# Two token-major projections in 512 columns, the second branch's gates ahead of the first branch's projection, and the attention heads six steps later

## The chip, the core and the metric

The kernel runs on one core of a Trainium2 chip. TensorE (PE) does the matrix products into eight banks of PSUM, ScalarE (ACT) and VectorE (DVE) move and transform the results, GpSimd (POOL) does some elementwise work that must not touch PSUM, and SyncE (SP) issues most of the DMA transfers. The metric is the device time of one execution in microseconds, the median of several runs. Only the order and the shape of work change here, not what is computed.

## The reference

Two transformer blocks over 256 tokens of width 1024, in fp32. The change touches the first block's mixer, cut here to what matters:

```python
hn = rmsnorm(h, norm_mix)
proj = hn @ w_in                      # 1024 x (many splits)
(fq, fk, fv, ff, gq, gk, gv, ga, gb, gz, gate_fox, gate_gdn) = split_in(proj)
y_fox = fox_attention(fq, fk, fv, log_sigmoid(ff + bias))     # 8 heads of 128, causal, forget gates
qkv = silu(causal_dwconv(concat(gq, gk, gv), gdn_conv_w))
o = gated_delta_rule(l2norm(q), l2norm(k), v, g, beta)         # 8 heads of 128
y_gdn = rmsnorm(o, gdn_norm) * silu(gz)
y = sigmoid(gate_fox) * (y_fox @ w_branch_fox) + sigmoid(gate_gdn) * (y_gdn @ w_branch_gdn)
h = h + y @ w_out
```

A feed-forward block with a short convolution follows, and then the second transformer block.

## The kernel before

Every weight matrix is read in **panels** of 1 MB (8 tiles of 128 rows by 256 columns, or 4 tiles of 128 rows by 512 columns). `panels()` writes the list `PLAN` out by hand, and its order is the order of the program. SyncE fetches a panel into one of three raw buffers. Each panel is worked on in two halves, the **steps**: there are 252, numbered n = 1 to 252, and everything is placed by n. To keep fp32 precision each half is split: ScalarE rounds it to `panel_hi` (L1019), VectorE subtracts to get `panel_lo` (L1469), and TensorE multiplies three times (high by high, low by high, high by low) in `gemm(n)` (L551). ScalarE's split of step n waits until TensorE has finished step n-4.

A panel has one of these forms. "fm" gives the product with features on partitions, "tm" with tokens on partitions: both are 24 matmuls of 256 columns in a step. "wide" gives tokens on partitions and 512 columns: 12 matmuls in a step, with two banks for a product. The gate `z` (z of `gz`) and the first attention's values `fv` are "tm" before; both have the normalised input `x_halves` as the stationary operand in either form.

All five engine programs are loops over n, and what an engine does beside the panels is hung on a step by conditions such as `if n == 68`. An engine works strictly in the order of its program. In the order of the program the steps before are: k, q, v, z for the delta rule (1 to 32); `fq`, `fk`, `fv` by turns (33 to 56); `gate_f` (57 to 64); `branch_f`, the projection of the first branch (65 to 72); `gate_g` (73 to 80); `branch_g` (81 to 88); `out` (89 to 96).

Hung on them, and named in the prediction:

- **The heads of the first attention**, from `FOX_AT = {39 + 3*hh: hh}`. For head hh with step s: TensorE computes the scores at s; VectorE adds `key_bias` and takes the maximum at s+1 (L1701); ScalarE exponentiates at s+2, and then issues the DMA load of the next head's key bias (L545, L546); VectorE normalises at s+3 (L1709, L1712); TensorE turns the probabilities at s+4 (`fox_turn`, L839) after waiting for that; TensorE multiplies by the values at s+5 (`fox_values`); ScalarE and VectorE split the result into `yf_hi` and `yf_lo` (L1717) at s+5. GpSimd adds the causal mask to head hh+1's `key_bias` (L2134) at its own position s+1, waiting for that load to land. There is one `key_bias` buffer.
- **The inversion of 16x16 blocks** for the delta rule: TensorE forms keys by keys at n = 38, VectorE inverts row by row from n = 42 to 47, the result goes to DRAM and back into `X` and `XT` (SyncE, n = 48), and TensorE needs `X` at n = 52 (`px_16`).
- **The solve** at n = 63 (`solve_first`, `solve_rest`), which gives `o_tok`. ScalarE squares it at n = 64, VectorE sums at 65 and takes the mean at 66; at n = 66 GpSimd raises the mean to the power -1/2 (L2129) and multiplies `o_tok` by `gz` (L2181); VectorE waits for this at n = 68, scales `o_tok` (L2006), and TensorE turns it at n = 71 (L674). GpSimd also scales and shifts the gates (L2140): `gate_f` at 58 to 64, `gate_g` at 74 to 80.
- **Banks.** Products up to `gate_f` use the ring "few" (banks 0 and 1), attention heads the ring "fox" (banks 2 and 3), later products the ring "gemm" (banks 0 to 3). A user of a bank waits until the one before it is emptied.

Of the kernel before, what the change touches and what calls it, by code (L numbers as in the profile page):

```python
# [19 lines left out]
ALU = mybir.AluOpType  # L20
# [50 lines left out]
for _name, _n in (("ident", P), ("upper", P), ("ones", 4), ("causal", P), ("decay_mask", P),  # L71
# [7 lines left out]
CONV_ORDER = [("k", 2), ("z", 0), ("k", 3), ("q", 0), ("z", 1), ("q", 1), ("q", 2), ("z", 2),  # L79
              ("q", 3), ("v", 0), ("z", 3), ("v", 1), ("v", 2), ("v", 3)]  # L80
# [8 lines left out]
def panels():  # L89
# [11 lines left out]
    for kind, j in CONV_ORDER:  # L101
# [49 lines left out]
SEQ = [("k", 0), ("k", 1)] + CONV_ORDER  # L151
CONVS = [p for p in SEQ if p[0] != "z"]
COPY_AT = {p: END[p] for p in SEQ} | {("k", 0): 4, ("k", 1): 5}
# [4 lines left out]
FOX_AT = {39 + 3 * hh: hh for hh in range(HEADS)}  # L158
# [31 lines left out]
def build(nc, a, out, scratch_a, scratch_x, scratch_c):  # L190
    ctx = ExitStack()
    with ctx:
# [35 lines left out]
        nwT = at("nwT", [P, HEADS, P], 11)  # L228
        S1 = at("S1", [P, HEADS, DH], 11.5)
# [8 lines left out]
        gate_g = at("gate_g", [P, KD, T], 18)  # L238
# [248 lines left out]

        def side(key):
            return bank_for("side", key)
# [59 lines left out]
        def tensor_program(e):  # L549
# [5 lines left out]
            def gemm(n):  # L555
# [286 lines left out]
            def fox_values(hh):  # L842
# [5 lines left out]
                e.wait_ge(*emptied(("fv", hh // 2)))  # L848
# [88 lines left out]
            for n in range(1, STEPS + 1):  # L937
# [41 lines left out]
                if n - 5 in FOX_AT and FOX_AT[n - 5] < 7:  # L979
# [8 lines left out]
                if n == 64:  # L988
                    fox_values(7)
# [27 lines left out]
        def scalar_program(e):  # L1017
# [101 lines left out]
            def z_tanh(j):  # L1119
                m = SEQ.index(("z", j))  # L1120
                tmp_free(m)
                e.wait_ge(*product(("z", j)))
                e.activation(conv_tmp[m % 4], pairs(bank_of(("z", j))), ACT.Tanh, scale=0.5).then_inc(s_gz_tanh, 1)
# [171 lines left out]
            for n in range(1, STEPS + 1):  # L1295
# [82 lines left out]
                if n - 5 in FOX_AT and FOX_AT[n - 5] < 7:  # L1378
# [7 lines left out]
                for j in range(4):  # L1386
# [10 lines left out]
                    if n == END["gate_g", j]:  # L1397
                        e.wait_ge(*emptied(("o1", 0)))
# [5 lines left out]
                if n == 64:  # L1404
                    fox_hi(7)
# [55 lines left out]
        def vector_program(e):  # L1461
# [74 lines left out]
            def z_silu(j, order):  # L1536
                e.wait_ge(s_gz_tanh, order)
                e.scalar_tensor_tensor(gz[:, :, col2(j)], conv_tmp[SEQ.index(("z", j)) % 4], 1.0,
                                       pairs(bank_of(("z", j))), ALU.add, ALU.mult).then_inc(empties(("z", j)), 1)
# [351 lines left out]
            for n in range(1, STEPS + 1):  # L1891
# [53 lines left out]
                if n in Z_AT:  # L1945
                    z_silu(Z_AT[n], Z_AT[n] + 1)
# [68 lines left out]
                if n - 5 in FOX_AT and FOX_AT[n - 5] < 7:  # L2015
# [19 lines left out]
                if n == 64:  # L2035
                    fox_lo(7)
# [346 lines left out]
```

## Time and profile before

| | us |
|---|---|
| median of 3 runs | 818.33 |
| lowest of 3 runs | 816.98 |
| the profiled execution | 817.55 |
| its span | 816.2 |

The profiled execution lies 0.78 us under the median. 1.35 us of it lie outside the span that the trace covers. TensorE is busy for 99% of the span, VectorE for 72%, ScalarE for 55% and GpSimd for 9%. So the time is close to what TensorE's instructions take one after another, and a microsecond counts where TensorE does less work or waits less. The granted clock is at its full level in the whole profile.

### The profile page before, as it was taken

Reading aid. Unit: us, or ns where it says so; the run is one execution under the profiler, and the core shown is the slowest. Engines: PE = TensorE matmul, PEld = TensorE weight load, DVE = VectorE, ACT = ScalarE, POOL = GpSimd, SP = SyncE. Lnnn points to the kernel's source line nnn. Section 1 sums busy time; section 2 is a strip of 40 time slices with the busy share of each in tenths; the row PEclk is TensorE's granted clock in tenths of the full one; section 3 lists DMA queues with packets and bytes.
Section 4 is the critical chain, followed back from the end, with each engine's and each line's share of the span. In section 5 each row is a group of like instructions: output and inputs, shape, how many; then the busy total and the mean of one; then the engine's idle time right before and its main releaser. Section 6 shows DMA issues by size and latency. Waiting matters only on the chain.

```text
span 816.2 us, 14536 instructions
## 1 busy us (share of the span) xinstructions
PE 804.7 (99%) x5910; PEld 738.6 (90%) x5910; DVE 589.5 (72%) x967; ACT 446.9 (55%) x721; POOL 76.6 (9%) x67
## 2 busy tenths in 40 slices
PE   7999999999999999999999999999999999999998
PEld 5999999999999999899999998888777888888886
DVE  6878878785553746669999997486766777777543
ACT  5666577654454444455656563456664656555441
POOL 0001000001010401100211011012100111011000
PEclk9999999999999999999999999999999999999999
DMA  8754663646440564575687766555424666565541
GB/s 261 234 172 143 192 223 109 181 136 186 116 134 31 163 199 162 200 232 167 198 244 223 240 199 208 185 185 177 155 78 132 207 203 203 173 192 193 192 162 72
DMA packets 130194, 144.18 MB, mean 177 GB/s; under 512 B 11456, under 2 KB 110928, under 8 KB 129872
## 3 DMA queue, kind: packets, MB, share of 16 engines
q1 hardware_dynamic: 127680, 141.19, 54.6%
q10 hardware_dynamic: 2448, 2.05, 1.0%
q8 instruction: 47, 0.77, 0.4%
q14 instruction: 19, 0.16, 0.1%
HBM read 141.78 MB, written 1.46 MB: 175 GB/s over the span
## 4 chain that ended last, share of the span: by engine, by line
PE 94%; DVE 2%; DMA 1%; ACT 1%; issue 0%; POOL 0%; ACTq 0%; DVEq 0%; POOLq 0%
PE bank L551 92%; DVE panel_lo L1469 1%; DMA panel_raw<-in_w_in 1%; PE bank L597 1%; DMA h<-in_x 1%; PE bank L889 0%; PE bank L619 0%; ACT panel_hi L1019 0%; PE bank L839 0%; DVE blocks_T L1628 0%; DVE decayT L1532 0%; PE bank L862 0%; PE bank L674 0%; DVE x_halves L1490 0%; DVE blocks_X L1631 0%
## 5 line engine op out<-in xcount | busy, mean ns | idle before, releaser
L1469 DVE TENSOR_TENSOR panel_lo<-panel_raw,panel_hi 128x1024 fp32r<-128x1024 f32 x252 | 319.3, 1270 | 153.4 <-ACT panel_hi L1019 153.1
L551 PE MATMUL bank<-x_halves,panel_hi 128*128 128x256 f32 (+1 forms) x1952 | 415.3, 304 | 1.7 <-DVE x_halves L1490 1.5
L1019 ACT ACTIVATE panel_hi<-panel_raw 128x1024 fp32r<-128x1024 f32 x252 | 266.6, 1059 | 176.7 <-PE bank L551 171.4
L551 PEld LDWEIGHTS bank<-x_halves,panel_hi 128*128 128x128 f32 x1952 | 315.3, 191 | 17.1 <-DVE panel_lo L1469 1.7
L551 PE MATMUL bank<-x_halves,panel_lo 128*128 128x256 f32 x1152 | 324.8, 282 | 0.0
L551 PEld LDWEIGHTS bank<-x_halves,panel_lo 128*128 128x128 f32 x1152 | 219.8, 191 | 0.0
L551 PE MATMUL bank<-panel_hi,x_halves 128*128 128x256 f32 (+1 forms) x384 | 88.1, 324 | 0.0
L551 PEld LDWEIGHTS bank<-panel_hi,x_halves 128*128 128x128 f32 x384 | 63.4, 190 | 5.8 <-issue 0.7
L551 PE MATMUL bank<-panel_hi,act_hi 128*128 128x512 f32 x176 | 68.6, 390 | 0.0
L551 PE MATMUL bank<-panel_hi,act_lo 128*128 128x512 f32 x176 | 68.5, 389 | 0.0
L551 PE MATMUL bank<-panel_lo,act_hi 128*128 128x512 f32 x176 | 68.5, 389 | 0.0
L551 PE MATMUL bank<-panel_lo,x_halves 128*128 128x256 f32 (+1 forms) x192 | 61.2, 319 | 0.0
L551 PEld LDWEIGHTS bank<-panel_hi,act_hi 128*128 128x128 f32 x176 | 33.0, 188 | 6.9
L551 PEld LDWEIGHTS bank<-panel_lo,act_hi 128*128 128x128 f32 x176 | 33.0, 188 | 6.9
L551 PEld LDWEIGHTS bank<-panel_hi,act_lo 128*128 128x128 f32 x176 | 33.0, 188 | 6.7
L551 PEld LDWEIGHTS bank<-panel_lo,x_halves 128*128 128x128 f32 x192 | 36.5, 190 | 2.6
L2129 POOL TENSOR_TENSOR stats<-stats 128x2 f32<-128x2 f32 (+1 forms) x9 | 17.1, 1906 | 190.1 <-DVE stats L1483 104.8
L1503 DVE SCALAR_TENSOR_TENSOR conv_acc<-conv_tmp,params,conv_acc 128x255 f32<-128x255 f32 (+2 forms) x72 | 30.2, 476 | 0.0
L2154 POOL TENSOR_TENSOR ff_tanh<-ff_tanh,ff_val 128x512 f32<-128x512 f32 x11 | 17.2, 1565 | 112.4 <-DVE ff_tanh L1780 112.4
L2161 POOL TENSOR_TENSOR f_tanh<-f_tanh,ff_val 128x512 f32<-128x512 f32 x11 | 14.3, 1299 | 108.3 <-DVE f_tanh L1856 108.3
L2134 POOL TENSOR_TENSOR key_bias<-key_bias,constants 128x128 f32<-128x128 f32 x16 | 8.9, 577 | 151.2 <-DMA key_bias<-gate_sums 151.2
L1774 DVE SCALAR_TENSOR_TENSOR ff_gate<-ff_raw,params,ff_gate 128x255 f32<-128x255 f32 (+1 forms) x44 | 21.3, 543 | 0.0
(284 smaller groups left out, 973.3 us busy)
## 6 DMA issues: line engine op xcount, KB each, us to landing
panel_raw<-in_w_in SPq DMA_DIRECT2D x38, 1024.0 KB, 5.3
panel_raw<-in_w_up SPq DMA_DIRECT2D x30, 1024.0 KB, 5.3
panel_raw<-in_w_down SPq DMA_DIRECT2D x20, 1024.0 KB, 5.1
panel_raw<-in_w_gate SPq DMA_DIRECT2D x10, 1024.0 KB, 5.3
panel_raw<-in_w_out SPq DMA_DIRECT2D x8, 1024.0 KB, 5.1
panel_raw<-in_w_in SPq DMA_DIRECT2D x12, 512.0 KB, 4.6
panel_raw<-in_w_branch_fox SPq DMA_DIRECT2D x4, 1024.0 KB, 5.2
panel_raw<-in_w_branch_gdn SPq DMA_DIRECT2D x4, 1024.0 KB, 5.1
```

The costliest lines, as they stand in the source:

```text
L551: return e.matmul(o, l, r, start=start, stop=stop, skip_group_check=True)
L597: i_ = e.transpose(b3[:, k, m * P:(m + 1) * P], h[:, m, f * P:(f + 1) * P], ident)
L1019: return e.activation(o, i_, ACT.Copy, scale=scale)
L1469: e.tensor_tensor(lo, raw_view(i, k0, kt), hi.bitcast(F32), ALU.subtract).then_inc(s_lo, 1)
L1503: e.scalar_tensor_tensor(acc[:, f, back:], tmp[:, f, 0:T - back], gconv(p, f, back), acc[:, f, back:], ALU.mult, ALU.add).then_inc(s_taps, 1)
L1774: e.scalar_tensor_tensor(acc[:, c, back:], raw_[:, c, 0:T - back], fconv(s, j, c, back), acc[:, c, back:], ALU.mult, ALU.add).then_inc(s_f ...
L2129: return e.tensor_tensor(cols, cols, minus_half.broadcast_to([P, n]), ALU.pow)
L2134: i_ = e.tensor_tensor(key_bias[:, s], key_bias[:, s], C("causal"), ALU.add)
L2154: e.tensor_tensor(th, th, ff_acc[j % 2][1], ALU.mult).then_inc(s_f_mul, 1)
L2161: e.tensor_tensor(th, th, ff_acc[j % 2][1], ALU.mult).then_inc(s_g_mul, 1)
```

## The change

The panels of `z` and of `fv` become "wide": four panels each of 4 row tiles by 512 columns, in the place of four panels of 8 row tiles by 256. The `z` panels keep their places among steps 7 to 26, and the products end at steps 14 and 26. The `fv` panels move in front of all of `fq` and `fk`, to steps 33 to 40. `fq` and `fk` follow at 41 to 56. Since queries and keys now end later, all heads start six steps later, at 45 to 66. `gate_g` moves in front of `branch_f`: `gate_g` has steps 65 to 72, `branch_f` 73 to 80. The last head, which ended with `fox_values(7)` at n = 64 directly behind its turn at n = 64, is now in the regular pattern (turn at 70, values at 71). The two matrices `nwT` and `S1` and the buffer `gate_g` change places in SBUF, so that `gate_g` no longer waits for the solve. A wide product takes two banks, and the wait for the second one stands just in front of the matmuls that write it.

```diff
-CONV_ORDER = [("k", 2), ("z", 0), ("k", 3), ("q", 0), ("z", 1), ("q", 1), ("q", 2), ("z", 2),
-              ("q", 3), ("v", 0), ("z", 3), ("v", 1), ("v", 2), ("v", 3)]
+CONV_ORDER = [("k", 2), ("z", 0), ("k", 3), ("q", 0), ("z", 0), ("q", 1), ("q", 2), ("z", 1),
+              ("q", 3), ("v", 0), ("z", 1), ("v", 1), ("v", 2), ("v", 3)]
...
-        add((kind, j), "mix", kind != "z", "w_in", 0, KD, c0 + j * PW)
+        if kind == "z":
+            add_wide((kind, j), "mix", "w_in", HALF * CONV_ORDER[:i].count((kind, j)), HALF, c0 + j * WIDE)
+        else:
+            add((kind, j), "mix", True, "w_in", 0, KD, c0 + j * PW)
+    for j in range(2):
+        for k in (0, HALF):
+            add_wide(("fv", j), "mix", "w_in", k, HALF, C_FV + j * WIDE)
     for j in range(4):
-        for kind, c0 in (("fq", C_FQ), ("fk", C_FK), ("fv", C_FV)):
-            add((kind, j), "mix", kind != "fv", "w_in", 0, KD, c0 + j * PW)
-    for kind, x, w, c0 in (("gate_f", "mix", "w_in", C_GF), ("branch_f", "yf", "w_branch_fox", 0),
-                           ("gate_g", "mix", "w_in", C_GG), ("branch_g", "yg", "w_branch_gdn", 0)):
+        for kind, c0 in (("fq", C_FQ), ("fk", C_FK)):
+            add((kind, j), "mix", True, "w_in", 0, KD, c0 + j * PW)
+    for kind, x, w, c0 in (("gate_f", "mix", "w_in", C_GF), ("gate_g", "mix", "w_in", C_GG),
+                           ("branch_f", "yf", "w_branch_fox", 0), ("branch_g", "yg", "w_branch_gdn", 0)):
...
-FOX_AT = {39 + 3 * hh: hh for hh in range(HEADS)}
+FOX_AT = {45 + 3 * hh: hh for hh in range(HEADS)}
...
-        nwT = at("nwT", [P, HEADS, P], 11)
-        S1 = at("S1", [P, HEADS, DH], 11.5)
+        nwT = at("nwT", [P, HEADS, P], 12)
+        S1 = at("S1", [P, HEADS, DH], 12.5)
...
-        gate_g = at("gate_g", [P, KD, T], 18)
+        gate_g = at("gate_g", [P, KD, T], 11)
...
+        def ring_of(key):
+            if key[0] == "z" or key in (("fv", 0), ("fq", 0), ("fk", 0)):
+                return "fox"
+            return "few" if END[key] <= END["gate_g", 3] else "gemm"
...
-                        bank_for("few" if n <= END["gate_f", 3] else "gemm", target)
-                        for s, v in room(target):
-                            e.wait_ge(s, v)
+                        bank_for(ring_of(key), target)
...
+                    if first and j < len(targets):
+                        for s, v in room(targets[j]):
+                            e.wait_ge(s, v)
...
-                e.wait_ge(*emptied(("fv", hh // 2)))
+                for m in range(TT):
+                    e.wait_ge(*emptied(("fv", hh // 4, m)))
...
-                if n - 5 in FOX_AT and FOX_AT[n - 5] < 7:
+                if n - 5 in FOX_AT:
                     fox_values(FOX_AT[n - 5])
...
-                if n == 64:
-                    fox_values(7)
...
-                        e.wait_ge(*emptied(("o1", 0)))
                         gate("gate_g", j, gate_g)
...
-                    if n == END["fv", j]:
-                        e.wait_ge(*product(("fv", j)))
-                        e.tensor_copy(vf[:, :, col2(j)], pairs(bank_of(("fv", j)))).then_inc(empties(("fv", j)), 1)
+                    if j < 2 and n == END["fv", j]:
+                        for m in range(TT):
+                            e.wait_ge(*product_of(("fv", j), m))
+                            e.tensor_copy(vf[:, m, wide(j)], bank_of(("fv", j, m))).then_inc(empties(("fv", j, m)), 1)
```

`z_tanh` (ScalarE) and `z_silu` (VectorE) do in the same way two instructions of 512 elements at n = 14 and two at n = 26, in the place of one at each of 8, 14, 20 and 26. Lines of the changed kernel are 14 to 16 numbers higher than those of the kernel before.

Three places where the order of an engine's instructions changes. First **GpSimd**, from the keys' norms to the second branch's gates. `key_bias` x2 is one head's mask, the `stats` row of 16 is the power, `o_tok` the multiplication by `gz`. Before:

```order
L2129 TENSOR_TENSOR stats<-stats 128x16
L2134 TENSOR_TENSOR key_bias<-key_bias,constants 128x128 x16
L2140 TENSOR_SCALAR gate_f<-gate_f 128x512 x4
L2129 TENSOR_TENSOR stats<-stats 128x16
L2181 TENSOR_TENSOR o_tok<-o_tok,gz 128x8x128 x2
L2140 TENSOR_SCALAR gate_g<-gate_g 128x512 x4
```

After:

```order
L2144 TENSOR_TENSOR stats<-stats 128x16
L2149 TENSOR_TENSOR key_bias<-key_bias,constants 128x128 x12
L2155 TENSOR_SCALAR gate_f<-gate_f 128x512 x2
L2149 TENSOR_TENSOR key_bias<-key_bias,constants 128x128 x2
L2155 TENSOR_SCALAR gate_f<-gate_f 128x512
L2149 TENSOR_TENSOR key_bias<-key_bias,constants 128x128 x2
L2155 TENSOR_SCALAR gate_f<-gate_f 128x512
L2144 TENSOR_TENSOR stats<-stats 128x16
L2197 TENSOR_TENSOR o_tok<-o_tok,gz 128x8x128 x2
L2155 TENSOR_SCALAR gate_g<-gate_g 128x512 x4
```

The masks of heads 6 and 7 have moved between the scalings of `gate_f`: the last one now stands behind two of them, and right in front of the last scaling and the power.

Second **VectorE**, from its step 65 on (before) and from its step 67 on (after), around the scaling of `o_tok`. `panel_lo` is the split of the next panel. Before:

```order
L1469 TENSOR_TENSOR panel_lo_60<-panel_raw_52,panel_hi_56 128x1024
L1996 TENSOR_REDUCE stats<-o_squares 128x8 x2
L1469 TENSOR_TENSOR panel_lo_57<-panel_raw_50,panel_hi_53 128x1024
L2000 SCALAR_TENSOR_TENSOR stats<-stats 128x16
L1724 TENSOR_TENSOR gate_f<-bank,gate_f 128x512
L1469 TENSOR_TENSOR panel_lo_58<-panel_raw_50,panel_hi_54 128x1024
L1469 TENSOR_TENSOR panel_lo_59<-panel_raw_51,panel_hi_55 128x1024
L2006 TENSOR_TENSOR o_tok<-o_tok,stats 128x1024 x2
L1724 TENSOR_TENSOR gate_f<-bank,gate_f 128x512
L1469 TENSOR_TENSOR panel_lo_60<-panel_raw_51,panel_hi_56 128x1024
```

After:

```order
L1483 TENSOR_TENSOR panel_lo_58<-panel_raw_50,panel_hi_54 128x1024
L1717 ISA fox_p_70,stats<-bank,key_bias 128x128
L1717 ISA stats 128x1
L1717 ISA fox_p_70,stats<-bank,key_bias 128x256
L1717 ISA stats 128x1
L1483 TENSOR_TENSOR panel_lo_59<-panel_raw_51,panel_hi_55 128x1024
L2022 TENSOR_TENSOR o_tok<-o_tok,stats 128x1024 x2
L1733 TENSOR_TENSOR yf_lo<-bank,yf_hi 128x256
L1483 TENSOR_TENSOR panel_lo_60<-panel_raw_51,panel_hi_56 128x1024
L1725 RECIPROCAL stats<-stats 128x2
L1728 TENSOR_SCALAR fox_p_70<-fox_p_70,stats 128x128
L1728 TENSOR_SCALAR fox_p_70<-fox_p_70,stats 128x256
```

Behind the scaling of `o_tok` there now follow head 6's `yf_lo`, a split, and the normalising of head 7 (RECIPROCAL and two TENSOR_SCALAR); before, all heads were done by then and only the products with `gate_f` followed.

Third **TensorE**, at the turn of head 7 (`fox_p_70`), which is after step 64 before and after step 70 now. Before:

```order
L551 MATMUL bank<-x_halves,panel_hi_56 128x256 x2
L551 MATMUL bank<-x_halves,panel_lo_60 128x256
L839 MATMUL bank<-constants,fox_p_70 128x128 x3
L551 MATMUL bank<-fox_pT_73,vf 128x128 x3
L551 MATMUL bank<-yf_hi,panel_hi_53 128x256
L551 MATMUL bank<-yf_lo,panel_hi_53 128x256
L551 MATMUL bank<-yf_hi,panel_lo_57 128x256
```

After:

```order
L566 MATMUL bank<-x_halves,panel_hi_54 128x256 x2
L566 MATMUL bank<-x_halves,panel_lo_58 128x256
L855 MATMUL bank<-constants,fox_p_70 128x128 x3
L566 MATMUL bank<-x_halves,panel_hi_55 128x256 x2
L566 MATMUL bank<-x_halves,panel_lo_59 128x256
```

The values of head 7 stood directly behind its turn; now a step of 24 matmuls and the turns of `o_tok` lie between them, and the turn itself stands six steps later, in front of the panel of `gate_g`.

## Rows read from the trace of the kernel before

**Rows 1.** The page: busy time, and shares of the chain that ended last.

```profile
PE 804.7 (99%) x5910; PEld 738.6 (90%) x5910; DVE 589.5 (72%) x967; ACT 446.9 (55%) x721; POOL 76.6 (9%) x67
...
PE 94%; DVE 2%; DMA 1%; ACT 1%; issue 0%; POOL 0%; ACTq 0%; DVEq 0%; POOLq 0%
```

**Rows 2.** Two stretches: length, busy time (count) of PE, PEld, DVE, ACT, POOL; PEclk, DMA.

```profile
400.00:480.00 80.00, 80.00 (x669) 80.00 (x668) 77.39 (x114) 47.77 (x70) 10.02 (x7) 1.00 0.74 227
760.00:810.00 50.00, 50.00 (x222) 41.41 (x221) 23.10 (x20) 17.59 (x18) 0.63 (x1) 1.00 0.43 141
```

**Rows 3.** Waits of TensorE over the whole span.

```profile
PE bank L619 <- DVE conv_tmp L1509: 1.0, 1, 1.0
PE bank L551 <- DVE stats L1701: 0.7, 1, 0.7
```

**Rows 4.** Timeline of TensorE: start, duration, instruction, idle before.

```profile
1.43 5.63 PE L551 MATMUL bank<-zeros 128*128 128x512 f32 x8 [1.43 <-DVE zeros L1863]
8.81 1.09 PE L597 MATMUL bank<-constants,h 128*128 128x128 f32 x8 [1.75 <-DVE h L1880]
...
188.98 2.06 PE L551 MATMUL bank<-X,BT 64*64 64x32 f32 x64
...
230.40 0.92 PE L551 MATMUL bank<-kfT,qfT 128*128 128x128 f32 x4
...
234.03 0.49 PE L839 MATMUL bank<-constants,fox_p 128*128 128x128 f32 x3
...
237.23 0.83 PE L551 MATMUL bank<-fox_pT,vf 128*128 128x128 f32 x6
...
240.78 1.06 PE L551 MATMUL bank<-tok_v,XT 128*128 128x128 f32 x8
...
259.54 0.49 PE L839 MATMUL bank<-constants,fox_p 128*128 128x128 f32 x3
260.78 0.91 PE L551 MATMUL bank<-fox_pT,vf 128*128 128x128 f32 x6 [0.75 <-issue]
```

**Rows 5.** Timeline of GpSimd, 225 to 277 us.

```profile
230.54 0.87 POOL L2134 TENSOR_TENSOR key_bias<-key_bias,constants 128x128 f32<-128x128 f32 x2 [12.47 <-DMA key_bias<-gate_sums]
231.38 1.30 POOL L2140 TENSOR_SCALAR gate_f<-gate_f 128x512 f32<-128x512 f32 x2
...
267.87 2.91 POOL L2129 TENSOR_TENSOR stats<-stats 128x16 f32<-128x16 f32 x1 [6.00 <-DVE stats L2000]
270.75 5.76 POOL L2181 TENSOR_TENSOR o_tok<-o_tok,gz 128x1024 f32<-128x1024 f32 x2
```

**Rows 6.** ScalarE issues the last key bias load; landing times of L546.

```profile
225.65 0.33 ACTq L545 DMA_DIRECT2D key_bias<-gate_sums  x1
...
DMA to landing us min/median/max: 4.3/4.5/7.2
```

**Rows 7.** Timeline of VectorE, 242 to 282 us.

```profile
242.56 0.15 DVE L1709 RECIPROCAL stats<-stats 128x2 f32<-128x2 f32 x1
242.75 0.55 DVE L1712 TENSOR_SCALAR fox_p<-fox_p,stats 128x128 f32<-128x128 f32 x2
...
262.14 0.42 DVE L1717 TENSOR_TENSOR yf_lo<-bank,yf_hi 128x256 fp32r<-128x256 f32 x1 [2.48 <-ACT yf_hi L1019]
...
276.61 2.36 DVE L2006 TENSOR_TENSOR o_tok<-o_tok,stats 128x1024 f32<-128x1024 f32 x2 [2.37 <-POOL o_tok L2181]
...
279.48 2.35 DVE L1469 TENSOR_TENSOR panel_lo<-panel_raw,panel_hi 128x1024 fp32r<-128x1024 f32 x2
```

**Rows 8.** VectorE around the block inversion, and the DMA issues behind it.

```profile
154.34 0.29 DVE L1960 TENSOR_SCALAR blocks_A<-blocks_A 128x256 f32<-128x256 f32 x1 [1.10 <-DMA blocks_A<-blocks_to_invert]
...
173.45 0.39 DVE L1970 COPY blocks_T<-blocks_X 128x256 f32<-128x256 f32 x1
...
L2278 SPq DMA_DIRECT2D X<-blocks_inverted x8: 319/448/450, 181.4 to 184.7; - x8
...
X<-blocks_inverted SPq DMA_DIRECT2D x8, 16.0 KB, 3.7
```

More of the change, by code:

```diff
@@ L149 @@
 FIRST_HALF = {p[0]: min(n for n, (i, _, _) in enumerate(HALVES) if PLAN[i][0] == p[0]) for p in PLAN}
-SEQ = [("k", 0), ("k", 1)] + CONV_ORDER
+SEQ = [("k", 0), ("k", 1)] + [q for i, p in enumerate(CONV_ORDER) if p not in CONV_ORDER[i + 1:]
+                              for q in ([(*p, m) for m in range(TT)] if p[0] == "z" else [p])]
 CONVS = [p for p in SEQ if p[0] != "z"]
-COPY_AT = {p: END[p] for p in SEQ} | {("k", 0): 4, ("k", 1): 5}
+COPY_AT = {p: END[p[:2]] for p in SEQ} | {("k", 0): 4, ("k", 1): 5}
 CONV_AT = {COPY_AT[p]: c for c, p in enumerate(CONVS)}
@@ L1119, in z_tanh @@
             def z_tanh(j):
[L1120 to L1123, printed above, removed]
+                for m in range(TT):
+                    i_ = SEQ.index(("z", j, m))
+                    tmp_free(i_)
+                    e.wait_ge(*product_of(("z", j), m))
+                    e.activation(conv_tmp[i_ % 4].rearrange("p c t -> p (c t)"), bank_of(("z", j, m)), ACT.Tanh, scale=0.5) \
+                        .then_inc(s_gz_tanh, 1)
             def turned(name, dst, b):
@@ L1377, in scalar_program @@
                              units(bank_of(("yg", b))), PR("gdn_norm")).then_inc(s_yg_hi, 1)
-                if n - 5 in FOX_AT and FOX_AT[n - 5] < 7:
+                if n - 5 in FOX_AT:
                     fox_hi(FOX_AT[n - 5])
@@ L1403, in scalar_program @@
                     px_32()
-                if n == 64:
-                    fox_hi(7)
                 for x, kind, gain, first in (("ffn", "out", "norm_ffn", 2), ("norm1", "down", "norm1", 4),
@@ L1534, in decay, with z_silu @@
                 i_.then_inc(s_dec_sub, 1)
[L1536 to L1539, printed above, removed]
+            def z_silu(j):
+                for m in range(TT):
+                    e.wait_ge(s_gz_tanh, 2 * j + m + 1)
+                    tanh = conv_tmp[SEQ.index(("z", j, m)) % 4].rearrange("p c t -> p (c t)")
+                    e.scalar_tensor_tensor(gz[:, m, wide(j)], tanh, 1.0, bank_of(("z", j, m)), ALU.add, ALU.mult) \
+                        .then_inc(empties(("z", j, m)), 1)
             def gates_1():
@@ L1945, in vector_program @@
                 if n in Z_AT:
-                    z_silu(Z_AT[n], Z_AT[n] + 1)
+                    z_silu(Z_AT[n])
                 if n == 38:
@@ L2014, in vector_program @@
                                                ALU.subtract).then_inc(empties(("yg", b)), 1)
-                if n - 5 in FOX_AT and FOX_AT[n - 5] < 7:
+                if n - 5 in FOX_AT:
                     fox_lo(FOX_AT[n - 5])
@@ L2021, in vector_program @@
                 for j in range(4):
-                    if n == END["fv", j]:
-                        e.wait_ge(*product(("fv", j)))
-                        e.tensor_copy(vf[:, :, col2(j)], pairs(bank_of(("fv", j)))).then_inc(empties(("fv", j)), 1)
+                    if j < 2 and n == END["fv", j]:
+                        for m in range(TT):
+                            e.wait_ge(*product_of(("fv", j), m))
+                            e.tensor_copy(vf[:, m, wide(j)], bank_of(("fv", j, m))).then_inc(empties(("fv", j, m)), 1)
                     if n == min(END["branch_g", j] + 1, END["branch_g", 3]) and j < 3:
@@ L2034, in vector_program @@
                     px_32()
-                if n == 64:
-                    fox_lo(7)
                 if n == 63:
@@ L2177, in pool_program @@
                     e.wait_ge(s_osq, 2)
-                    for j in range(4):
-                        e.wait_ge(*emptied(("z", j)))
+                    for j in range(2):
+                        for m in range(TT):
+                            e.wait_ge(*emptied(("z", j, m)))
                     for m in range(TT):
```

2 lines of the change are left out of this document (1 added, 1 removed).

## The prediction

> **What bounds the kernel now.** I read the page first. TensorE is busy for 804.7 us of the 816.2 us span, and 94% of the chain that ended last are its own instructions [rows 1]. So TensorE is the bound nearly everywhere, and there are only two ways to move the time: make its work shorter, or change how long it waits. The other engines matter where they make it wait. The list of waits says how little there is to win: in the steps that change, the longest are one of 1.0 us for `conv_tmp` and one of 0.7 us for `stats` L1701 [rows 3], and a few under 1 us that have no engine's name. Next I read what a step costs in each form. In 80 us of 256-column steps there lie 669 matmuls, in 50 us of 512-column steps 222 [rows 2]. Such a count takes in two or three matmuls that only reach into the stretch, so the true distance from one to the next is a little over 80/669 and 50/222: 0.120 and 0.227 us, with the count corrected by 2. Last I read the timelines of the four engines between 225 and 282 us, where the last heads, the solve and the scaling of `o_tok` meet [rows 4 to 7], and around the block inversion [rows 8].
>
> **Part 1, 512 columns.** A step of 24 matmuls by 0.120 is 2.88 us, one of 12 by 0.227 is 2.72 us [rows 2]. The bytes, the splits and the columns stay equal: only 12 fixed costs of a matmul go. 16 steps (8 of `z`, 8 of `fv`) by 0.16 us give **-2.5 us**. In both stretches TensorE is busy all the time and the weights' loading (80.00 of 80, 41.41 of 50) does not hold it, with `x_halves` or the other operand as the stationary one; I take the 0.16 whole. The bounds are nothing and -2.5. The Trainium skill, in "TensorE: Matmul & The Clock Gate", section "Wait — 56ns, not 53.3ns?", puts a warm matmul at its columns over 2.4 GHz plus about 2.5 ns. By that a step of either form would take 2.62 or 2.59 us and this part would give 0.5 us, not 2.5; the trace has some 13 ns over the columns for each matmul, so it does not agree, and the measured distance is used.
>
> **Part 2, evacuations.** The four tanh and four products of `z` are 512 elements each, as before, but two fall together at n = 14 and at n = 26; the same with the copies of `fv`, at 36 and 40. They are not on TensorE and the panels run several microseconds ahead. One place is thinner: TensorE waits 1.0 us for the gated `conv_tmp` at n = 37 [rows 3], where VectorE works without a break. VectorE's chain is set off by the turns of step 33, TensorE comes four short steps sooner: I add +0.1 us, at most +0.6. The changed order of the banks costs nothing: each bank has at least four steps between its uses.
>
> **Part 3, the heads six steps on.** Six is a multiple of three, so between steps 45 and 63 the same kind of head work stands in each step as before, only of a head two lower. TensorE's work for a head is the same wherever it stands. From the starts in the timeline: scores to turn 3.63, turn to values 3.20, values to the next 3.55 us, each with a step of 2.88 in it, so 0.75 + 0.32 + 0.67 = 1.74 us [rows 4]. What changes is where it waits.
> - Head 7's turn and values stood back to back after step 64: the turn took 1.24 us to the start of the values, which waited 0.75 for the copy of the turned probabilities, where a turn costs 0.32 [rows 4]. Now a step lies between. That gives **-0.9 us**.
> - The wait of 0.7 us for `stats` L1701 [rows 3] came from a head's bias queued on VectorE behind the inversion (n = 46), at 171 us. The head work in the inversion's steps is now less, so I take it as gone: **-0.7 us** (bounds 0 and -0.7).
> - The inversion's results must be back when TensorE reaches `px_16` at 188.98 [rows 4]. TensorE will be there sooner by 2.5 + 0.7 and by the work of two heads, 3.3 to 3.5 us: about 6.4 us. The way back starts sooner as well: VectorE spent 154.34 to 173.45 on the inversion [rows 8], and in it 3.3 us on heads 0 and 1 and on a copy of `fv`, which are no longer there; with another 2 us for the start (a shorter way to the keys by keys, one copy of `fv` less in front of them) the result leaves 5.3 us sooner. The way back, through DRAM, ended with the eighth issue of `X` at 184.7 and 3.7 us for its landing [rows 8]: `X` was back at 188.4, 15 us after the inversion, with 0.6 us to spare. 0.6 + 5.3 - 6.4 is -0.5 at the middle. I take **+0.3 us**, between 0 and +2.
>
> **Part 4, the new wait.** This decides. I count from the start of the solve, 240.78 [rows 4], as 0; up to there all engines keep their distances. Step 64 ends at 18.8 (259.54), and with head 6's scores now behind the solve at 19.4. TensorE would go on: turn 5, step 65 to 22.6; values 5, step 66 to 26.2; scores 7, step 67 to 29.7; turn 6, step 68 to 32.9; values 6, step 69 to 36.4; step 70 to 39.3. There it wants to turn head 7, for which VectorE must have normalised it.
> - VectorE stands still before that, at n = 68, until GpSimd has multiplied `o_tok` by `gz` (it idles 2.37 us for it even now) [rows 7]. Behind that wait are queued the scaling of `o_tok`, `yf_lo` of head 6, the split of step 72 and only then the normalising of head 7.
> - GpSimd in turn has got head 7's mask in front of the power. The load of that key bias is issued when ScalarE reaches the values of head 5, at 22.6 + 0.7 = 23.3; the mask began 4.9 us after the issue (225.65 to 230.54), as soon as both halves had landed [rows 5, 6], so at 28.2. With 0.87 for the mask and 0.65 for one scaling of `gate_f` the power can start at 29.7, where its own input would allow 27.3 (27.1 before, and 0.2 for the heads' work on VectorE). The power takes 2.9 (267.87 to 270.75), the two products 5.76 [rows 5]: 38.4.
> - VectorE then: 2.36 for `o_tok`, 0.35 of the 0.42 for `yf_lo`, 1.17 for the split, 0.65 for reciprocal and two scalings [rows 7] (each but the last up to where the next begins): 43.0.
> TensorE waits from 39.3 to 43.0: **+3.7 us**. The lower bound is no mask in the way: 2.4 less, +1.3. The upper: the second half of such a load landed after 4.5 us in the median and after 7.2 at most [rows 6]; with 7.2 the wait is +6.4. Nothing is late behind it: the split of step 72 is done at 42.3 and wanted at 46; `yf_lo` of head 7 at about 50.5 and wanted for step 74, at 54. The squares of `o_tok` come as early as before against the solve.
>
> **Part 5, gates.** `gate_g` runs the same matmuls in the same form 8 steps sooner, with ScalarE's tanh in the place of VectorE's products. Its scaling on GpSimd stands behind the multiplication of `o_tok`, as before. Nothing waits: 0, covered by the eight steps of `branch_f` until `branch_g` wants it.
>
> **The sum.** -2.5 + 0.1 - 0.9 - 0.7 + 0.3 + 3.7 = 0.0. On the profiled execution's 817.55 us (span 816.2 and 1.35 outside) that is 817.6; its own median is 818.33, 0.8 above it. I forecast 818.0, between the two: **no change**, what the wide panels give being taken back by the wait at head 7's turn. A difference of under 2% (16 us) can't be told from none.
>
> **Rivals.**
> - *The wait is hidden* (chance 0.22). If GpSimd's chain is done some 3 us sooner, or VectorE starts `o_tok` sooner, TensorE finds head 7 ready: 817.6 - 3.7, about 814. For it: two of GpSimd's numbers are rough, and the power's 2.9 us may be start-up. Against it: even without the mask the chain ends 1.3 us too late.
> - *The load of the key bias lands late* (0.13), on the other side: VectorE's wait grows one for one with the landing. At 7.2 us in the place of 4.5 it gives 817.6 + 2.7 = 820.3, and the kernel is slower than before as soon as the load needs half a microsecond more than in the median. For it: one of the loads here did need 7.2 [rows 6]. Against it: the last one, in the same traffic of panels, was at the median.
> - *The clock falls* (0.10). A wait of 3.7 us would be the longest of TensorE. In this trace it waited up to 1.75 us with the clock still at its full level, 2.4 GHz, after [rows 4]. Only the first matmuls, after nothing, were slow: 5.63 us for 4 products of 512 columns, while four products of 128 columns take 1.06 us with the last one's tail [rows 4], so that four of 512 should take about 4. A drop to 1.2 GHz would then cost some 1.7 us: 819.3. The same page of the Trainium skill, section "What's actually happening", has the array fall back to 1.2 GHz after enough idleness; no row here shows such a fall.
> - *Wide steps give nothing* (0.05): if the half as many matmuls keep the same total, as the columns do, the 2.5 us are missing: 817.6 + 2.5 = 820.1. Against it speak the two counts of rows 2, made in the same kernel. (By the Trainium skill's rule of part 1, same page, 0.5 of them would be left and the time 819.6.)
>
> **How the numbers follow.** The forecast's case (a wait of 2.5 to 5.5 us, 816 to 819.5) has 0.50. The range takes in the hidden wait below and the late load above, with 0.8 us between median and profiled run at the top: 813.5 to 821.5. All cases lie within 2% (802 to 835): same 0.98, and 0.01 on each side for what I have not seen.
>
> **What the profile would show.** 12 matmuls in 2.72 us in the steps of `z` and `fv`. TensorE idle for 3 to 5 us in front of the `fox_p` turn that stands one step ahead of the turns of `o_tok`, ended by VectorE L1728, with GpSimd's mask late in front of its power. No 0.75 us wait in front of the last values. At `px_16` a wait under 2 us. I am wrong if there is no such wait, or if a wait of several microseconds stands elsewhere, above all at `px_16` or in front of a panel.

## The result, and the profile after

The changed kernel takes 821.11 us in the median of 6 runs (820.67 to 822.02), the kernel before 817.65 in the median of the 5 beside them (816.98 to 819.08), with one execution of 1600.22 left out (817.99 with it). The ratio is 1.004, with a 95% interval of 1.0028 to 1.0051: over 3 us slower. That is inside 2%, but outside what the runs scatter. The profiled execution took 820.71 us, with a span of 819.4.

The page of the changed kernel, its busy times and the chain that ended last; then three lines from the list of TensorE's waits (us in total, times, longest), the longest and those at the places of [rows 3] and of px_16:

```profile
PE 804.2 (98%) x5718; PEld 729.9 (89%) x5718; DVE 589.2 (72%) x967; ACT 446.8 (55%) x721; POOL 76.2 (9%) x67
...
PE 88%; issue 4%; DVE 3%; DMA 3%; POOL 1%; ACT 1%; SPq 0%; ACTq 0%; POOLq 0%; DVEq 0%
```

```profile
PE bank L855 <- DVE fox_p L1728: 4.9, 1, 4.9
...
PE bank L635 <- DVE conv_tmp L1523: 1.3, 1, 1.3
...
PE bank L566 <- DMA X<-blocks_inverted: 0.3, 1, 0.3
```

The wait that was forecast is there, at the turn of head 7, and it is now the longest of TensorE by far: 4.9 us. Against [rows 1], TensorE's part of the chain falls from 94% to 88%. Of these six points GpSimd and VectorE have taken one each and DMA two; the 4% of "issue" are not lost time but mostly one piece of 25.99 us, in which the chain runs through GpSimd's idle time in front of head 7's mask while TensorE works. The chain around that place shows in which order (start, length, what):

```profile
238.87 25.99 issue
...
264.90 0.09 POOL key_bias L2149
...
265.31 0.46 POOL key_bias L2149
265.77 0.59 POOL gate_f L2155
266.37 2.87 POOL stats L2144
269.23 4.76 POOL o_tok L2197 x2
...
274.08 3.10 DVE o_tok L2022 x2
277.18 0.34 DVE yf_lo L1733
277.52 1.13 DVE panel_lo L1483
278.65 0.09 DVE stats L1725
...
278.76 0.56 DVE fox_p L1728 x2
...
279.45 0.69 PE bank L855 x3
```

The timeline of TensorE from px_16 to the turns of `o_tok`. The solve, which answers to 240.78 in [rows 4], starts at 235.03, px_16 (188.98 there) at 183.09:

```profile
183.09 2.06 PE L566 MATMUL bank<-X,BT 64*64 64x32 f32 x64 [0.28 <-DMA X<-blocks_inverted]
...
235.03 1.06 PE L566 MATMUL bank<-tok_v,XT 128*128 128x128 f32 x8
...
274.23 0.28 PE L566 MATMUL bank<-x_halves,panel_lo 128*128 128x256 f32 x1
279.45 0.69 PE L855 MATMUL bank<-constants,fox_p 128*128 128x128 f32 x3 [4.95 <-DVE fox_p L1728]
279.80 0.78 PE L566 MATMUL bank<-x_halves,panel_hi 128*128 128x256 f32 x2
280.37 0.41 PE L566 MATMUL bank<-x_halves,panel_lo 128*128 128x256 f32 x1
...
283.12 0.40 PE L566 MATMUL bank<-x_halves,panel_hi 128*128 128x256 f32 x2
283.36 0.28 PE L566 MATMUL bank<-x_halves,panel_lo 128*128 128x256 f32 x1
...
284.19 1.91 PE L690 MATMUL bank<-constants,o_tok 128*128 128x128 f32 x16
```

Behind the wait, from 279.80 to 283.12, the matmuls stand 0.21 us apart; from 283.12 on it is the usual 0.12. The windows of the same place show why (length; busy and count of PE, PEld, DVE, ACT, POOL; granted clock; DMA):

```profile
278.00:280.00 2.00, 0.55 (x4) 0.58 (x5) 1.97 (x5) 0.00 (x0) 0.00 (x0) 0.91 0.09 22
280.00:282.00 2.00, 2.00 (x11) 2.00 (x11) 0.44 (x1) 1.75 (x3) 0.62 (x1) 0.50 0.99 343
282.00:284.00 2.00, 2.00 (x15) 2.00 (x14) 1.23 (x1) 0.17 (x1) 0.00 (x0) 0.73 0.46 160
284.00:286.00 2.00, 2.00 (x20) 2.00 (x20) 0.46 (x1) 1.18 (x3) 0.00 (x0) 1.00 0.71 226
```

The granted clock is 0.50, 1.2 GHz, from the end of the wait until about 283.1 (what the windows lack to 1.00 adds up to 3.4 us at half the clock). Where the time went is read from the end of each step (the moment at which TensorE reports its products), before and after, side by side. The changed kernel is 0.12 us late after step 1, 1.16 ahead after step 26 (all of `z`), 5.75 ahead after step 57, 4.46 ahead after step 70, with head 7's turn and values (0.99 us) still to come. Step 71 then takes 9.84 us; with 2.88 for its products and 0.32 for the turn it would be 3.20. The 6.64 us over are 4.95 of waiting and 1.69 behind it. From step 72 to the end the distance stays between 3.1 and 3.2.

### The profile page after: what moved, and what is told of

It is laid out like the page before. It is cut to its first block, busy times and chain, and to the rows that moved or that the text cites. A ratio compares the mean times of both kernels' runs of the same rounds, so it can differ in the third digit from the quotient of the medians.

```text
span 819.4 us, 14145 instructions
## 1 busy us (share of the span) xinstructions
PE 804.2 (98%) x5718; PEld 729.9 (89%) x5718; DVE 589.2 (72%) x967; ACT 446.8 (55%) x721; POOL 76.2 (9%) x67
## 4 chain that ended last, share of the span: by engine, by line
PE 88%; issue 4%; DVE 3%; DMA 3%; POOL 1%; ACT 1%; SPq 0%; ACTq 0%; POOLq 0%; DVEq 0%
PE bank L566 85%; DVE panel_lo L1483 1%; DMA blocks_inverted<-blocks_X 1%; PE bank L613 1%; DMA h<-in_x 1%; POOL o_tok L2197 1%; DMA X<-blocks_inverted 1%; DMA key_bias<-gate_sums 1%; PE bank L906 0%; PE bank L635 0%; POOL stats L2144 0%; DVE o_tok L2022 0%; ACT panel_hi L1034 0%; SPq L2294 0%; DVE blocks_T L1644 0%
## 5 line engine op out<-in xcount | busy, mean ns | idle before, releaser
L566 PE MATMUL bank<-panel_hi,x_halves 128*128 128x512 f32 x256 | 80.6, 396 | 0.0
L566 PEld LDWEIGHTS bank<-panel_hi,x_halves 128*128 128x128 f32 x256 | 46.8, 188 | 9.9 <-DVE panel_lo L1483 0.6
L566 PE MATMUL bank<-panel_lo,x_halves 128*128 128x512 f32 x128 | 50.0, 391 | 0.0
L566 PEld LDWEIGHTS bank<-panel_lo,x_halves 128*128 128x128 f32 x128 | 24.0, 188 | 5.2
```

The source lines that it names most:

```text
L566: return e.matmul(o, l, r, start=start, stop=stop, skip_group_check=True)
```

## The experiments

The profiles differ in their start: step 1 ends at 14.6 to 14.9 us in seven of the twelve traces and at 16.1 to 16.3 in five. Most of that is TensorE's clock. It starts on `x_halves` at 11.4 to 11.8 us in all of them, but in the five the granted clock is at 0.50 for 3.4 us around that start. The kernel without wide `z` of the last experiment shows it:

```profile
8.90 1.09 PE L607 MATMUL bank<-constants,h 128*128 128x128 f32 x8 [2.12 <-DVE h L1886]
11.52 0.68 PE L560 MATMUL bank<-x_halves,panel_hi 128*128 128x256 f32 x2 [1.52 <-DVE x_halves L1496]
```

```profile
10.00:12.00 2.00, 0.48 (x3) 0.51 (x4) 1.98 (x5) 2.00 (x5) 0.00 (x0) 0.91 1.00 314
12.00:14.00 2.00, 2.00 (x11) 2.00 (x11) 1.99 (x5) 1.88 (x4) 0.00 (x0) 0.50 0.00 1
```

So each experiment at head 7 is read from step 71 alone, and the medians stand beside it. The table holds all of them; the last column is what is left of step 71 when the idle time and the extra products are taken from it and the 3.20 us of its own work too.

| kernel | median, runs | ratio to before, interval | step 71 | extra products | idle | clock after | left |
|---|---|---|---|---|---|---|---|
| changed | 821.11 (6) | 1.0040, 1.0028 to 1.0051 | 9.84 | 0 | 4.95 | 0.50 | 1.69 |
| scaling behind | 816.20 (11) | 0.9978, 0.9970 to 0.9987 | 4.82 | 0 | 1.42 | 1.00 | 0.20 |
| power in front | 818.49 (12) | 1.0005, 0.9995 to 1.0016 | 5.98 | 0 | 2.60 | 1.00 | 0.18 |
| 36 extra | 830.80 (4) | 1.0154, 1.0140 to 1.0167 | 18.75 | 15.55 | 0 | 1.00 | 0 |
| 15 extra | 821.13 (5) | 1.0035, 1.0022 to 1.0048 | 9.67 | 6.47 | 0 | 1.00 | 0 |
| 8 extra | 820.14 (8) | 1.0033, 1.0019 to 1.0047 | 8.31 | 3.5 | 1.45 | 1.00 | 0.2 |
| 4 extra | 822.23 (5) | 1.0044, 1.0032 to 1.0056 | 9.61 | 1.7 | 3.17 | 0.50 | 1.5 |
| both orders | 815.49 (5) | 0.9966, 0.9954 to 0.9978 | 3.20 | 0 | 0 | 1.00 | 0 |

**The scaling of `o_tok` behind the normalising of head 7.** VectorE's block of n = 68 (wait for `s_ogz`, scaling) is moved:

```diff
-                if n == 68:
+                if n == 69:          # now below fox_normalise and fox_bias
                     e.wait_ge(s_o_rs, 1)
                     e.wait_ge(s_ogz, 2)
```

> The changed kernel with one edit: VectorE's scaling of o_tok (which waits for GpSimd's product with gz) stands behind the normalising of head 7 instead of in front of it. Theory A (the whole loss is the 4.95 us of idle TensorE in front of the turn of head 7, together with the lower clock that follows it): step 71 goes from 9.84 us to 3.2, nothing is late behind it (the scaling ends near 277.2, its turn is reached near 277.7), and the time falls by 4.95 + 1.69 = 6.6 us, to about 814.1 for the profiled execution and 814.5 in the median, 0.996 of the kernel before. Rival B (the wait moves on to the turn of the scaled o_tok, since the scaling now stands behind two more pieces of work): half or more of the 6.6 us stays, 817 to 820. Rival C (the slow clock belongs to this place and not to the wait): only 4.95 us come back, about 816.2.

Measured: 816.20, and step 71 shorter by 5.02 us, not 6.64. The slow stretch is gone with the long wait, against rival C. Rival B did not happen either: nothing waits at the turn of `o_tok`. A wait of 1.42 us stayed, at the same turn, for a reason that no theory named. VectorE and GpSimd in that kernel:

```profile
274.60 0.15 DVE L1725 RECIPROCAL stats<-stats 128x2 f32<-128x2 f32 x1
274.79 2.86 DVE L1728 TENSOR_SCALAR fox_p<-fox_p,stats 128x128 f32<-128x128 f32 x2
```

```profile
271.18 5.74 POOL L2197 TENSOR_TENSOR o_tok<-o_tok,gz 128x1024 f32<-128x1024 f32 x2
276.89 1.24 POOL L2155 TENSOR_SCALAR gate_g<-gate_g 128x512 f32<-128x512 f32 x2
```

The two small scalings take 2.86 us where they took 0.55 [rows 7]: VectorE stands until GpSimd's product is over, at 276.92. Without these 2.31 us head 7 would have been ready before TensorE wanted it, at 276.4. The Trainium skill, in "SBUF — State Buffer", section "Who interferes with whom", says that the two engines share a pair of ports, that a scaling by a scalar can take both of VectorE's, and that whoever comes second is blocked until the other's instruction is done. The trace agrees, with 2.86 us for 0.55.

**The power in front of the mask.** On GpSimd:

```diff
+    mask_key_bias(7)                 # in the block of n == 66, behind power(...)
-    if n - 1 in FOX_AT and FOX_AT[n - 1] + 1 < HEADS:
+    if n - 1 in FOX_AT and FOX_AT[n - 1] + 1 < HEADS - 1:
```

> The changed kernel with one edit on GpSimd: the power for o_tok stands in front of the mask of head 7, and no longer waits for the load of that key bias. The prediction put the share of the mask and its load at 2.4 us. From the trace of the changed kernel: the power's input is there at 262.1 and it starts at 266.3; it would start at 262.1, end at 265.0, mask to 265.9, gate_f to 266.5, the products to 271.3, and head 7 would be normalised near 276.5. Theory A: the wait shrinks from 4.95 to about 2 us; as no wait of up to 1.75 us was followed by a lower clock, the clock stays full and 1.7 us more come back: 820.7 - 3.0 - 1.7 = 816.0 (817.7 if the clock falls all the same). Rival B (GpSimd is not what VectorE waits for): no change, 821.

Measured: a wait of 2.60 us, the clock at 1.00 behind it, step 71 shorter by 3.86. GpSimd is what VectorE waits for, and the mask and its load in front of the power made the wait 2.35 us longer (4.95 less 2.60), even after the 1.0 us by which the products are slower here. The median, 818.49, fell by 2.6 only, over a wide scatter of 12 runs (816.80 to 822.08). That fits a clock that sometimes falls behind this wait too: one stretch of 3.4 us at half the clock takes 0.002 off the mean granted clock, the traces have at most one such stretch at the start, and four of the 12 executions have a mean of 0.993 to 0.996. They took 819.09 to 822.08 us, the four with a mean of 1.00 took 816.80 to 818.11. Where their clock fell isn't shown, since only the profiled execution has a trace. GpSimd's rows in this kernel:

```profile
263.60 2.91 POOL L2144 TENSOR_TENSOR stats<-stats 128x16 f32<-128x16 f32 x1 [5.44 <-DVE stats L2016]
266.47 0.88 POOL L2149 TENSOR_TENSOR key_bias<-key_bias,constants 128x128 f32<-128x128 f32 x2
267.31 5.76 POOL L2198 TENSOR_TENSOR o_tok<-o_tok,gz 128x1024 f32<-128x1024 f32 x2
273.04 2.17 POOL L2155 TENSOR_SCALAR gate_g<-gate_g 128x512 f32<-128x512 f32 x2
```

The products take 5.76 us again, as before the change; in the changed kernel, where VectorE does nothing beside them, 4.78.

**Extra products in the wait.** In front of TensorE's wait for the normalised head 7:

```diff
+                if hh == 7:
+                    for _ in range(36):      # 15, 8, 4 in the others
+                        mm(bank[:, 0:T], qfT[:, hh, 0:P], kfT[:, hh, :])
                 e.wait_ge(s_fox_norm, hh + 1)
```

> The changed kernel with 36 extra products of TensorE (qfT by kfT of head 7, 256 columns, overwritten by the turn that follows) in front of its wait for the normalised head 7; they compute nothing that is used. The work and the wait of the other engines are unchanged. Theory A (after the idle stretch TensorE runs at 1.2 GHz for some 3.5 us, which costs 1.7 us): the turn starts at the same time, near 279.4, but at full clock, and the time falls by 1.7, to 819.4 in the median. Rival B (the slow stretch comes from something else, for example the panel transfers that start again together): the granted clock still falls after 279.4 and the time stays at 821.1.

> As the run with 36 extra products, with 15 of them: TensorE is busy for the first 1.8 us of its wait and idle for the last 3.1. It asks where between 1.75 us (idle, clock still full in the kernel before) and 4.95 us (idle, clock halved in the changed kernel) the clock falls, at an unchanged total wait. If it falls: 821.1, with some 3.5 us at half clock. If it stays: 819.4. I expect that it falls (0.6).

Both runs were built on a wrong size: one extra product takes 0.43 us (15 of them 6.47), not 0.12, since the trace holds two matmuls for each, 0.22 us apart. TensorE in the run with 15:

```profile
275.00 6.64 PE L566 MATMUL bank<-kfT,qfT 128*128 128x256 f32 x30
281.47 0.49 PE L858 MATMUL bank<-constants,fox_p 128*128 128x128 f32 x3
```

So even 15 last longer than the wait, and neither answers the question that it was made for. They answer another one: 36 and 15 extra products make step 71 exactly as long as its own 3.20 us and theirs (15.55 and 6.47), with nothing left. With 15 of them TensorE reaches head 7's turn 1.5 us later than the data are there, and the step still ends 0.17 us sooner than in the changed kernel. So 1.69 us are lost behind the wait only where TensorE was idle in it. With that, the rival that the clock falls at this place whatever TensorE did is out.

> The changed kernel with 8 extra products of TensorE in front of its wait for head 7, nothing used of them. 15 of them turned out to take 6.5 us, 0.43 each, so 8 take 3.5 us: they fit into the wait of 4.95 us and leave 1.5 us idle. Theory A (the idle stretch itself costs 1.69 us more in lower clock): the wait ends at the same time, the clock stays full after it, step 71 goes from 9.84 to 8.15 and the median to 819.4. Rival B (the clock would have fallen anyway): 821.1.

> As the run with 8 extra products, with 4: 1.7 us busy, then 3.2 us idle. The run with the power in front had 2.60 us idle and the clock at full level after it, the changed kernel 4.95 us and half. It asks on which side 3.2 us lies: 819.4 if the clock stays, 821.1 if it falls. I expect that it stays (0.6).

With 8, the wait ends as expected and the clock stays full: step 71 is 8.31 us, 1.53 less than in the changed kernel (1.69 were expected; 0.2 us behind a wait stay even at full clock, as the last column shows for three kernels). The median, 820.14, falls by 1.0, and the intervals overlap, so it is the trace that decides. With 4, the clock fell, against what I expected:

```profile
281.30 0.90 PE L858 MATMUL bank<-constants,fox_p 128*128 128x128 f32 x3 [3.17 <-DVE fox_p L1731]
281.86 0.78 PE L566 MATMUL bank<-x_halves,panel_hi 128*128 128x256 f32 x2
282.43 0.41 PE L566 MATMUL bank<-x_halves,panel_lo 128*128 128x256 f32 x1
```

```profile
280.00:282.00 2.00, 0.70 (x4) 0.70 (x4) 1.97 (x5) 0.00 (x0) 0.00 (x0) 0.70 0.10 15
282.00:284.00 2.00, 2.00 (x11) 2.00 (x11) 0.38 (x1) 1.70 (x3) 0.62 (x1) 0.50 0.99 342
```

At this place waits of 1.42, 1.45 and 2.60 us had the full clock behind them in the traces, waits of 3.17 and 4.95 us half of it for 3.4 us, which cost 1.3 and 1.5 us beside the 0.2. But the length of a single wait doesn't decide it. At the start of the program TensorE waits for `h`, works for 1.09 us and waits 1.53 us more: the seven traces with a first wait of 0.86 to 1.75 us kept the full clock behind the second, the five with 2.12 to 2.52 us lost it, and none of these waits is as long as the 2.60 us that had no such effect at head 7. What does decide isn't shown. These traces say only that two waits close together can cost what one long wait costs.

**Both orders together.** The two edits above in one kernel.

> The changed kernel with both edits: on GpSimd the power in front of the mask of head 7, on VectorE the scaling of o_tok behind the normalising of head 7. With the scaling alone moved, TensorE still waited 1.42 us, and the two small scalings of fox_p took 2.86 us in the place of 0.55, while GpSimd multiplied o_tok by gz. Theory A (the two engines block each other when they work at the same time): with the power in front, GpSimd's product ends near 273.1, before head 7 is normalised near 274.8, and TensorE wants it at 276 (both for a start like that of the run with the power in front); the wait is gone, step 71 takes 3.2 us, and the median is 821.1 - 6.6 = 814.5. Rival B (the normalising is late for another reason, such as the exponentials of ScalarE): 1.4 us of wait stay and the median is that of the run with the scaling moved alone, 816.2.

Measured: no wait at head 7's turn, step 71 3.20 us, 6.64 less than in the changed kernel, as computed. The median is 815.49, 0.9966 of the kernel before: faster than both. It fell by 5.6 us and not by 6.6; in the traces 0.7 us of this is a longer wait in step 56 (1.03 for 0.31 us), of which more below. VectorE's rows there:

```profile
273.47 0.15 DVE L1725 RECIPROCAL stats<-stats 128x2 f32<-128x2 f32 x1
273.66 1.10 DVE L1728 TENSOR_SCALAR fox_p<-fox_p,stats 128x128 f32<-128x128 f32 x2
274.68 2.34 DVE L2035 TENSOR_TENSOR o_tok<-o_tok,stats 128x1024 f32<-128x1024 f32 x2
```

The scaling of `fox_p` is no longer behind the product (it is beside the two short scalings of `gate_g`, and takes 1.10 us). Rival B is out.

**The gates alone**, on the kernel before:

```diff
-    ("gate_f", ...), ("branch_f", ...), ("gate_g", ...), ("branch_g", ...)
+    ("gate_f", ...), ("gate_g", ...), ("branch_f", ...), ("branch_g", ...)
```

> The kernel before with one part of the change alone: the panels of gate_g in front of those of branch_f; the heads, the 256-column steps and head 7's turn and values stay where they were. The prediction put this part at 0 us, on the ground that it runs the same matmuls and nothing waits for it: 818.0, within 0.5 us of the kernel before. Rival: the tanh of gate_g on ScalarE in the steps of the last heads, or GpSimd's scaling of gate_g beside VectorE's scaling of o_tok, holds up head 7 or the o_tok turn and costs 1 us or more.

Measured: 817.55, ratio 1.0000 (0.9992 to 1.0009). The trace has a new wait of 0.3 us, but for head 0's `fox_p`, at 157.48 us and before any step that the edit moves. Nothing of it is left at step 57 or at the end of the span. The rival's hold-up at head 7 or at the turn of `o_tok` isn't there, and the part costs nothing.

**Wide `z` alone, and everything but wide `z`.** The first is the kernel before with the edits of `CONV_ORDER`, `add_wide` for `z`, its tanh and its product; the second is the kernel with both orders, with those edits undone.

> The kernel before with one part of the change alone: z in steps of 512 columns (its tanh and product two at n = 14 and two at n = 26); the values, the heads and the gates stay as they were. The prediction put a step of 512 columns at 0.16 us less than one of 256: 8 steps give 1.3 us, and in the trace of the changed kernel these eight steps were 1.12 us shorter in sum. Theory A: the steps after n = 26 stand 1.1 us earlier, and at the end of the span 1.1 us is left, 816.9 in the median. Rival B (the gain is given back behind it, since the copies of values and the taps are released by panels that come no earlier): no change, 818.0.

> The changed kernel with both edits of order (power in front of the mask, scaling of o_tok behind the normalising), and with z back in steps of 256 columns: the first part of the change half undone. Alone on the kernel before, wide z gave nothing, because TensorE then waited 0.89 us at px_16 for X and 0.67 us more in step 56. The question is whether wide z pays in the changed kernel. Theory A (in both kernels TensorE arrives at px_16 about when X does; with z narrow it arrives 1.1 us later, the inversion on VectorE starts about 1.1 us later too, and X is no earlier): the wide z is worth what the steps save, 1.1 us, and the median is 815.5 + 1.1 = 816.6. Rival B (X's way back is the bound at that place in both, and TensorE's narrow steps only fill the wait): 815.5, no wait at px_16.

Measured: 818.60 (12 runs; ratio 1.001, 1.0000 to 1.0021) for wide `z` alone, so it gives nothing that can be seen (817.75 for its five executions with a mean granted clock of 1.00, 818.02 for the 13 of the kernel before), and 814.70 (5 runs; 0.9963, 0.9950 to 0.9977) for the other, so its absence costs nothing. In the traces the eight steps are 1.1 us shorter in the one and 1.1 us longer in the other, just as the change's are. The time is given back between steps 53 and 57. In the kernel with wide `z` alone:

```profile
188.71 2.06 PE L563 MATMUL bank<-X,BT 64*64 64x32 f32 x64 [0.89 <-DMA X<-blocks_inverted]
...
209.60 0.50 PE L563 MATMUL bank<-panel_hi,x_halves 128*128 128x256 f32 x2 [0.67 <-issue]
```

VectorE had ended the inversion 1.2 us sooner than in the kernel before (172.22 for 173.45 in [rows 8]) and the last load of `X` was issued 1.75 us sooner, but it was back no sooner: 188.57 for 188.35, since it took 5.6 us to land for 3.6. Why isn't shown. In the other pair px_16 waits 0.2 to 0.3 us with either width, and it is the second place that takes the gain: the kernel with both orders waits 1.03 us in step 56 with no engine or transfer shown as the cause, its twin with narrow `z` not at all. Of the nine kernels with wide `z` all have this wait (0.31 to 1.04 us). Of the three with narrow `z` two have none, and the kernel before has 0.20 a little further on, in the burst of small matmuls behind step 56. So theory A of the last run had the steps right and the end wrong. The time, 814.70, is on rival B's side (815.5, against 816.6), but not by its mechanism: the wait that took the gain is not the one at px_16.

## Why the prediction was wrong

- **Part 1, 512 columns: right in the steps, too large in the time.** The eight steps of `z` save 1.12 us, 0.14 each for the 0.16 forecast; those of `fv` 0.09 to 0.16 each where no head stands in them. Part of it is lost again by the wait in step 56, 0.31 us in the profiled execution, 1.0 in most of the others. I had not reckoned with a wait there, and its cause stays open.
- **Part 2, `conv_tmp`: right**, +0.3 us, between my +0.1 and the bound of +0.6.
- **Part 3, the heads: right.** The wait for `stats` and the 0.75 us in front of the last values are gone, px_16 waits 0.28 us for the +0.3 forecast. All three parts together: 4.46 us ahead after step 70, less the 0.99 of head 7 still to do, is 3.5 us won; the sum of the prediction up to there was 3.7.
- **Part 4, the new wait: the failed step.** The mechanism was right, and so was the place; the term was too small. Forecast +3.7, measured +6.64: a wait of 4.95, and 1.69 behind it, which the sum had at nothing. Counted from the start of the solve, TensorE came at 39.5 (forecast 39.3) and head 7 was normalised at 44.3 (43.0). The mask came 1.7 us late (29.9 for 28.2), of which 1.4 come from the second half of that key bias: it took 5.9 us to land, where the median of [rows 6] is 4.5. The transfers issued from 255 to 262 us (KB each, us to landing) show what stood beside it, a panel of 1024 KB:

```profile
panel_raw<-in_w_branch_fox SPq DMA_DIRECT2D x1, 1024.0 KB, 6.3
key_bias<-gate_sums ACTq DMA_DIRECT2D x1, 128.0 KB, 5.9
```

  That panel was issued at 258.24, 0.65 us before the second half (258.89). The kernel before had this pattern twice: halves issued at 149.65 and 172.79, with a panel issued at 150.40 and 172.55, had their masks start 5.7 and 7.2 us later. With the nearest panel over 2 us away it was 4.3 to 4.6 us for the other five heads whose load ScalarE issued, the last one (226.01, panel at 223.18) among them. So the argument of the prediction that the last load had landed at the median "in the same traffic" was a misreading: the change moved the load next to the issue of a panel. That the panel is the cause is argued from these cases; no run moved the one against the other.

  GpSimd's products gave 1.0 back (4.78 for 5.76, since VectorE stood), and VectorE's scaling took 0.7 more (3.10 for 2.36), beside GpSimd's scaling of `gate_g`. Durations taken from [rows 5] and [rows 7] were those of engines that had other neighbours.
- **The rivals.** The clock (0.10) came true, with the price given for it, 1.7 us, as an addition to a longer wait; half of the rival of the late load (0.13) as well (1.4 us of 2.7). I had held them for alternatives to my forecast and to each other. But the later a load, the longer the wait, and the longer the wait, the likelier the fall: the cases belong together on one side, and together they make 3.7 + 1.25 + 1.69 = 6.64. That the price of the fall met 1.7 so closely is in part luck: 0.2 of the 1.69 also stay behind waits with the full clock. With the row of 1.75 us as the longest wait with full clock behind it, a forecast wait of 3.7 was well beyond what any row covered, and 0.10 was too little. That wide steps give nothing (0.05) is untrue of the steps and true of the time of `z` by itself.
- **Part 5, the gates: right**, 0.

So the forecast of no change failed by one link: the wait at head 7's turn, its length by 1.25 us and its after-effect by 1.69. The range, 813.5 to 821.5, took the time in all the same, but the kernel got 3 us slower where no change was forecast.

## What to carry to other kernels

Before heads, tiles or panels are moved, list what is queued behind each wait of an in-order engine: here one small normalising stood behind a wait for another engine's long product, and two moved pieces turned 3 us lost into 2.5 gained. Price a forecast wait together with what follows it, the clock included, once it is longer than any wait in the trace, or once two waits stand close together. Look at what other transfer a moved load will be issued beside. And a saving of work ahead of a place where TensorE waits for something else is not a saving until TensorE is seen to pass that place earlier.

## What the runs showed of the hardware

- At head 7's turn TensorE's clock was at 2.4 GHz behind waits of 1.42, 1.45 and 2.60 us and at 1.2 GHz behind those of 3.17 and 4.95 us, there for 3.4 us. At the start it was also at 1.2 GHz behind two waits of 2.12 to 2.52 and 1.53 us with 1.09 us of work between them (five traces), and not where the first was 1.75 us or less (seven). The Trainium skill, in "TensorE: Matmul & The Clock Gate", section "What's actually happening", has the array fall back to its lower clock when it has been idle; the windows of 0.50 above agree. The waits of 1.42, 1.45 and 2.60 us left 0.2 us behind them at full clock.
- VectorE and GpSimd were slower beside each other: two scalings 2.86 for 0.55 us, the products with `gz` 5.76 for 4.78 us, the scaling of `o_tok` 3.10 for 2.36, and the split of a panel beside the products 2.72 for 1.23 (kernel before, at 271.51).
- A key bias load of 128 KB that ScalarE issued within 0.75 us of a panel of 1024 KB was back after 5.6 to 7.2 us, one with no panel that near after 4.1 to 5.1 (kernels before and after).
- In step 56, behind two bursts of 64 small matmuls, TensorE waits 0.31 to 1.04 us in all kernels with wide `z`, and in none of the three without. The DMA queue for instructions moves packets in that stretch, so a late supply of instructions is a possible cause; none of the runs shows it, and why the form of steps that lie 30 to 50 steps earlier should matter stays open.
